# First norm by blocks in the input stage, and five sixths of the modulation weights loaded and multiplied inside the differential heads

## The chip, the cores and the metric

One core of a Trainium2 chip runs the whole program. The metric is the device time of one execution in microseconds (us), lower is better; a comparison is made between runs of two kernels on the same chip.

## The reference, cut to what matters

A two-layer trunk works on 1,024 latent tokens and 128 context tokens of width 1,024, in float32. Layer 0 mixes tokens by differential attention (8 heads), layer 1 by grouped-query attention; each is followed by a gated feed-forward with a short convolution. All norms are modulated:

```python
def adaln_params(cond, mod_w, mod_b):
    m = jax.nn.silu(cond) @ mod_w + mod_b
    return jnp.split(m[:, None, :], N_MOD, axis=-1)
def modulate(x, norm_w, shift, scale):
    return rms_norm(x, norm_w) * (1.0 + scale) + shift
def layer(x, cond, l, rope, ctx_kv):
    sh_a, sc_a, g_a, sh_f, sc_f, g_f = adaln_params(cond, mod_w[l], mod_b[l])
    o, k, v = token_mixer(modulate(x, norm_attn[l], sh_a, sc_a), l, rope, ctx_kv)
    x = x + g_a * o
    f = conv_ffn(modulate(x, norm_ffn[l], sh_f, sc_f), w_up[l], conv_w[l], conv_b[l], w_down[l])
    return x + g_f * f, k, v
```

`mod_w` is 2 x 1,024 x 6,144 floats (48 MB), multiplied with two conditioning vectors. Before the first attention only the shift and scale of the first norm are needed, the first third of layer 0's columns. The first gate is needed after the differential attention, the rest later.

## The kernel before, in words

The program is a row of stages (`build`, L135): `phase_input`, `phase_norm(g, 0)`, `phase_diff_attention`, a trunk stage, the second attention, a second trunk stage. Each stage has one instruction list for each engine: TensorE (PE), VectorE (DVE), ScalarE (ACT), GpSimd (POOL) and SyncE (SP, which issues DMAs). Each list is executed in its order; semaphores tie the engines together, and a stage ends with a barrier.

**Modulation (`phase_input`, L203).** SP loads `mod_w` in 48 slices of 1 MB: six parts ("sixths") `s` of 2,048 columns, each in 8 slices `k` of 128 rows (L244), four buffers in turn. PE multiplies each slice with the conditioning column in four matmuls of 32 x 512 side by side in one PSUM bank (L313). After 8 slices ACT copies the sum, PE transposes it and DVE adds the bias (L345). Between the parts PE transposes the tokens (L299) that POOL loads.

**First norm (`phase_norm`, L371).** Squares on ACT, their sums on DVE, a root on POOL, then `Hh` (ACT, L392) and `Hl` (POOL, L428), the high and low halves of the normed input, for all 1,152 tokens at a time.

**Products.** A float32 product is three matmuls (`product`, L450): high times high, low times high, high times low. Weights arrive in `g.wr`, ACT rounds them to `g.wh` (`w_hi`, L1358), POOL subtracts to get `g.wl` (`w_lo`, L1453). One bank is 24 matmuls of 128 x 384 (`linear_bank`, L457), and a projection (q, k or v of one head) has three banks, ("W", x, n).

**Heads (`phase_diff_attention`, L1195).** `first` computes k, q, v of head 0 and a bank of head 1; then each head is a `body` of ten steps, `s` = 0 to 9. In a step PE does the scores of token tile `s` (`scores_by_rows`, L1560), the transposes of the probabilities of tile `s-1` ("T", L1186), one projection bank of the next head, and in some steps weighted values ("PV"), mean squares ("ST"), broadcasts of roots ("BC"), transposes of cached and new keys. All but the scores use two PSUM banks in turn; `Ring` (L66) numbers the uses, and `wait_free` waits until the use two earlier has been read out. DVE does maxima, rotary steps (`rope`) and `combine` (the difference of the two softmaxes). ACT does exponentials and read-outs. POOL does, in this order within a step:

```python
for s in range(STEPS):
    for p in ST_AT.get(s, []):       # s = 3, 5, 7, 9
        root(ring, p)                # waits for DVE's mean square
    for p in BC_AT.get(s - 1, []):   # s = 5, 7, 9
        store(ring, h, p, not ahead)
    if ahead and s in (1, 4):
        w_lo(after(h, 1), W_HI_AT[s])
    if ahead2 and s == 7:
        w_lo(after(h, 2), "k")
```

ACT does `w_hi` at the end of its steps 1, 4 and 7, behind the read-out of that step's projection bank. The heads 0 to 5 are three rounds of a loop (`Fori`) over two heads, so their waits compare with registers; heads 6 and 7 stand behind it. `g.wr` has two slots, filled in turn. The keys and queries are rotated through two buffers, `rk` and `rq`, that DMAs fill with swapped halves (`rope_swap`, L1131).

Of the kernel before, what the change touches and what calls it, by code (L numbers as in the profile page):

```python
# [134 lines left out]
def build(nc, a):  # L135
# [3 lines left out]
    g.nc, g.a, g.stack, g.norm_sems = nc, a, ctx, {}  # L139
    with ctx:  # L140
# [8 lines left out]
        g.mod = sb("mod", [P, 2 * NMOD, 2])  # L149
        g.coef = sb("coef", [P, 4, KC, 2])  # L150
# [50 lines left out]


def phase_input(g):  # L203


    nc, a, PS = g.nc, g.a, g.PS
    b, stack = scope(g, "in", {
        "rows": ([P, 5, P], F32), "xn": ([P, 3, D], F32), "sc": ([P, KC, 32], F32),
        "mw": ([P, 4, 2048], F32), "mrow": ([P, 2, 512], F32), "lrow": ([P, 4, DH], F32),
        "lprod": ([P, 2, DH], F32), "lsum": ([P, 2], F32), "lexp": ([P, 2], F32)},  # L210
        "zeroed rows_in lam_in x_in0 x_in1 x_in2 mw0 mw1 mw2 mw3 const par_t par_e silu x_t x_e mw_used mod_row mod_t mod_e coef"
        " lam_steps lam_exp", reused=True)
    xin = [b.x_in0, b.x_in1, b.x_in2]
    mw_in = [b.mw0, b.mw1, b.mw2, b.mw3]
    with stack, nc.Block() as block:
        @block.sync
        def _(sp):
            sp.wait_ge(b.zeroed, 1)
            R = b.rows
            loads = [  # L220
                (R[PC_C:PC_C + 8, 0, :], a.c.rearrange("b (k p) -> (b k) p", p=P)),
                (R[PC_CTX:PC_CTX + 8, 0, :], a.c_ctx.rearrange("(k p) -> k p", p=P)),
                (R[PC_NA:PC_NA + 16, 0, :], a.norm_attn.rearrange("l (k p) -> (l k) p", p=P)),
                (R[PC_NF:PC_NF + 16, 0, :], a.norm_ffn.rearrange("l (k p) -> (l k) p", p=P)),
                (R[PC_FIN:PC_FIN + 8, 0, :], a.final_norm.rearrange("(k p) -> k p", p=P)),
                (R[PC_SUB:PC_SUB + 1, 0, :], a.subln_diff),
                (R[PC_QN:PC_QN + 1, 0, 0:DH], a.q_norm_gqa), (R[PC_QN:PC_QN + 1, 0, DH:P], a.q_norm_gqa),
                (R[PC_KN:PC_KN + 1, 0, 0:DH], a.k_norm_gqa), (R[PC_KN:PC_KN + 1, 0, DH:P], a.k_norm_gqa),
                (R[0:96, 1, :], a.mod_b.rearrange("l (k p) -> (l k) p", p=P)),
            ]  # L230
# [16 lines left out]
        @block.scalar  # L247
        def _(act):
            act.wait_ge(b.par_e, 1)
            for cond, col in ((0, PC_C), (1, PC_CTX)):  # L250
                last = act.activation(b.sc[:, :, cond], g.par[:, col:col + KC], ACT.Silu)
            last.then_inc(b.silu, 1)
            for s in range(6):
                act.wait_ge(b.mw_used, KC * (s + 1))
                if s >= 2:
                    act.wait_ge(b.mod_t, s - 1)
                act.activation(b.mrow[:, s % 2, :], PS[:, 2 + s % 2, :], ACT.Copy).then_inc(b.mod_row, 1)
            act.wait_ge(b.lam_steps, 3)
            act.activation(b.lexp[:, :], b.lsum[:, :], ACT.Exp).then_inc(b.lam_exp, 1)

        @block.gpsimd
        def _(pool):
            pool.memset(b.rows[:, :, :], 0.0).then_inc(b.zeroed, 1)
            pool.memset(g.ident[:, :], 0.0).then_inc(b.const, 1)
            pool.memset(b.sc[:, :, :], 0.0).then_inc(b.const, 1)
            pool.memset(g.ones_d[:, :], 1.0 / D).then_inc(b.const, 1)
            pool.memset(g.ones_v[:, :], 1.0 / P).then_inc(b.const, 1)
            pool.memset(g.half[:, :], -0.5).then_inc(b.const, 1)
            pool.memset(g.ones_h[:, :], 0.0).then_inc(b.const, 1)
            pool.memset(g.one[:, :], 1.0).then_inc(b.const, 1)  # L270
            pool.wait_ge(b.const, 7)
            pool.affine_select(out=g.ident[:, :], in_=g.ident[:, :], compare_op=ALU.not_equal, fill=1.0,
                               base=0, pattern=[[-1, P]], channel_multiplier=1).then_inc(b.const, 1)
            pool.wait_ge(b.const, 8)
            pool.memset(g.ones_h[0:DH, 0:1], 1.0 / DH).then_inc(b.const, 1)
            pool.wait_ge(b.const, 9)
            pool.memset(g.ones_h[DH:P, 1:2], 1.0 / DH).then_inc(b.const, 1)

            for t in range(TT):
                if t >= 3:  # L280
                    pool.wait_ge(b.x_t, 2 * (t - 2))
                src = a.x_sample[0, t * P:(t + 1) * P, :] if t < QT else a.x_prompt[0, :, :]
                pool.dma_start(b.xn[:, t % 3, :], src).then_inc(xin[t % 3], 16)

        @block.tensor
        def _(pe):
            pe.wait_ge(b.const, 10)
            pe.wait_ge(b.rows_in, 16 * 15)
            for i in range(5):
                last = pe.transpose(PS[:, i // 4, (i % 4) * P:(i % 4 + 1) * P], b.rows[:, i, :], g.ident[:, :])  # L290
            last.then_inc(b.par_t, 1)

            def x_tile(t):
                pe.wait_ge(xin[t % 3], 16 * (t // 3 + 1))
                for hf in range(2):
                    if t:
                        pe.wait_ge(b.x_e, 2 * (t - 1) + hf + 1)
# [4 lines left out]

            for t in range(3):
                x_tile(t)
            pe.wait_ge(b.silu, 1)
            for s in range(6):
                if s >= 2:
                    pe.wait_ge(b.mod_row, s - 1)
# [2018 lines left out]
```

## Time and profile before

| | before |
|---|---|
| median of 3 runs | 3683.11 us (3680.57 to 3684.28) |
| profiled execution, its own time | 3682.36 us |
| its span, first to last instruction | 3680.7 us |
| TensorE matmuls busy | 3358.0 us (91%) |
| VectorE / ScalarE / GpSimd busy | 1834.0 (50%) / 1181.1 (32%) / 963.7 us (26%) |
| mean granted TensorE clock | 0.949 of full speed |
| read from / written to HBM | 181.79 / 31.98 MB |

The own time holds 1.7 us around the span. In the profile, "idle before" is the time in which an engine waited ahead of an instruction, with the instruction of another engine that released it; the granted clock is 1.00 at 2.4 GHz and 0.50 at 1.2 GHz. Matmul ends are modelled and overlap, so the distance of two starts is the better measure of their pace.

### The profile page before, as it was taken

What the parts mean: (1) busy time and instruction counts of PE and PEld (TensorE: products, weight loads), DVE (VectorE), ACT (ScalarE), POOL (GpSimd) and SP (SyncE); (2) the same over time, 40 slices, a digit from 0 to 9 for tenths busy, and PEclk for the clock granted to TensorE, in tenths of its full rate; (3) what the DMA queues carried; (4) which work ended last, traced back from release to release, by engine and by line L of the source; (5) the groups of instructions that cost most, each with busy time, mean ns of one, the idle gap of its engine ahead of it and who ended that gap; (6) DMA issues with size and microseconds to landing.
All of it is one profiled execution on the core that took longest, in us unless ns stands there. A gap on an engine that the chain in (4) does not pass through costs nothing. (4 is left out here: it accounts for less than half of the span.)

```text
span 3680.7 us, 52758 instructions
## 1 busy us (share of the span) xinstructions
PE 3358.0 (91%) x20815; PEld 3086.4 (84%) x20815; DVE 1834.0 (50%) x2580; ACT 1181.1 (32%) x2085; POOL 963.7 (26%) x732
## 2 busy tenths in 40 slices
PE   5469999998799999999988899999898999999997
PEld 1168888887699999999988777877688999999996
DVE  0345555555335555545545455555516554555554
ACT  0224444444323122221224455555513212122121
POOL 0122222222142233222324122222133322233221
PEclk7689999999899999999999999999899999999998
DMA  9621111111311111111102211111221111111101
GB/s 386 268 61 47 44 45 45 45 45 55 143 36 57 41 40 42 49 36 38 40 29 84 50 30 28 30 26 36 98 92 42 55 42 40 34 40 51 40 29 58
DMA packets 200897, 229.80 MB, mean 62 GB/s; under 512 B 29924, under 2 KB 172893, under 8 KB 194461
## 3 DMA queue, kind: packets, MB, share of 16 engines
q1 hardware_dynamic: 192733, 204.64, 17.3%
q0 software_dynamic: 7856, 22.29, 1.7%
q8 instruction: 122, 2.00, 0.2%
q10 hardware_dynamic: 144, 0.52, 0.0%
q14 instruction: 42, 0.34, 0.0%
HBM read 181.79 MB, written 31.98 MB: 58 GB/s over the span
## 5 line engine op out<-in xcount | busy, mean ns | idle before, releaser
L452 PE MATMUL psum<-Hh,wh 128*128 128x384 f32 x3360 | 1141.3, 340 | 73.8 <-POOL wl L1453 38.2
L454 PE MATMUL psum<-Hl,wh 128*128 128x384 f32 x3360 | 1129.9, 336 | 0.0
L453 PE MATMUL psum<-Hh,wl 128*128 128x384 f32 x3360 | 1129.7, 336 | 0.0
L533 DVE SCALAR_TENSOR_TENSOR x<-psum,mod,x 128x384 f32<-128x384 f32 (+2 forms) x768 | 377.3, 514 | 686.1 <-PE psum L454 642.0
L452 PEld LDWEIGHTS psum<-Hh,wh 128*128 128x128 f32 x3360 | 636.2, 189 | 83.3 <-POOL wl L1453 38.5
L453 PEld LDWEIGHTS psum<-Hh,wl 128*128 128x128 f32 x3360 | 636.1, 189 | 0.0
L454 PEld LDWEIGHTS psum<-Hl,wh 128*128 128x128 f32 x3360 | 635.7, 189 | 0.0
L827 POOL TENSOR_TENSOR wl<-wr,wh 128x1024 fp32r<-128x1024 f32 x88 | 219.7, 2496 | 986.6 <-ACT wh L746 986.6
L777 ACT ACTIVATE ff_u<-psum 128x768 f32<-128x768 f32 x88 | 71.6, 813 | 1109.1 <-PE psum L454 1109.1
L452 PE MATMUL psum<-ff_ah,ff_dh 128*128 128x384 f32 x1056 | 365.2, 346 | 29.4 <-POOL ff_al L849 20.7
L975 DVE SCALAR_TENSOR_TENSOR ff_c<-ff_u,par,ff_c 128x1153 f32<-128x1153 f32 x176 | 377.3, 2144 | 15.7 <-DVE ff_c L972 5.2
L454 PE MATMUL psum<-ff_al,ff_dh 128*128 128x384 f32 x1056 | 357.0, 338 | 0.0
L453 PE MATMUL psum<-ff_ah,ff_dl 128*128 128x384 f32 x1056 | 356.7, 338 | 0.0
L452 PEld LDWEIGHTS psum<-ff_ah,ff_dh 128*128 128x128 f32 x1056 | 199.4, 189 | 47.6 <-POOL ff_al L849 21.3
L2246 DVE TENSOR_REDUCE ga_nm<-psum 128x1 f32<-128x1152 f32 x144 | 177.9, 1235 | 113.3 <-PE psum L2121 113.3
L1604 DVE TENSOR_REDUCE da_nb<-psum 128x1 f32<-128x1152 f32 x144 | 171.6, 1233 | 112.1 <-PE psum L1560 112.1
L972 DVE TENSOR_SCALAR ff_c<-ff_u,par 128x1153 f32<-128x1153 f32 x88 | 81.9, 931 | 286.4 <-ACT ff_u L779 286.4
L2134 PE MATMUL psum<-ident,ga_e 128*128 128x128 f32 x1168 | 182.1, 303 | 39.1 <-ACT ga_e L1957 35.7
L2134 PEld LDWEIGHTS psum<-ident,ga_e 128*128 128x128 f32 x1168 | 142.3, 153 | 78.8 <-ACT ga_e L1957 44.7
L453 PEld LDWEIGHTS psum<-ff_ah,ff_dl 128*128 128x128 f32 x1056 | 200.3, 190 | 0.0
L454 PEld LDWEIGHTS psum<-ff_al,ff_dh 128*128 128x128 f32 x1056 | 199.8, 189 | 0.0
L1957 ACT ACTIVATE ga_e<-psum,ga_nb,ga_r 128x1152 f32<-128x1152 f32 x144 | 174.8, 1216 | 43.4 <-DVE ga_nb L2250 40.3
(208 smaller groups left out, 4216.0 us busy)
## 6 DMA issues: line engine op xcount, KB each, us to landing
in_mw<-mod_w SPq DMA_DIRECT2D x48, 1024.0 KB, 8.8
wr<-w_up SPq DMA_DIRECT2D x88, 512.0 KB, 3.9
ff_dr<-w_down SPq DMA_DIRECT2D x22, 1024.0 KB, 6.0
wr<-w_qkv_diff SPq DMA_DIRECT2D x24, 512.0 KB, 3.9
x<-x_save SPq DMA_DIRECT2D x16, 576.0 KB, 9.1
Hh<-oh_save SPq DMA_DIRECT2D x14, 576.0 KB, 9.6
Hl<-ol_save SPq DMA_DIRECT2D x14, 576.0 KB, 10.5
x_save<-x_a SPq DMA_DIRECT2D x1, 4608.0 KB, 13.6
```

The costliest lines, as they stand in the source:

```text
L452: pe.matmul(out, w_hi, m_hi, start=start, stop=False)
L453: pe.matmul(out, w_lo, m_hi, start=False, stop=False)
L454: return pe.matmul(out, w_hi, m_lo, start=False, stop=stop)
L533: last = dve.scalar_tensor_tensor(g.x[:, m, lo:hi], g.PS[:, bank, lo - n * NB:hi - n * NB], g.mod[:, gate + m, cond:cond + 1], g.x[:, m, l ...
L777: act.activation(u[:, 1:1 + 2 * NB].rearrange("p (n t) -> p n t", n=2), PS[:, s:s + 2, 0:NB], ACT.Copy)
L827: pool.tensor_tensor(g.wl[:, j % 2, :, :], g.wr[:, j % 2, :, :], g.wh[:, j % 2, :, :].bitcast(F32), ALU.subtract).then_inc(b.w_lo, 1)
L972: dve.tensor_scalar(c, u[:, 0:PADT], tap(0), bias, ALU.mult, ALU.add).then_inc(b.conv, 1)
L975: dve.scalar_tensor_tensor(c, u[:, step:step + PADT], tap(step), c, ALU.mult, ALU.add).then_inc(b.conv, 1)
L1604: dve.reduce_max(b.nb[:, m:m + 1], banks(g, m, t), AX.XY if t < QT else AX.X, negate=True).then_inc(b.nmax, 1)
L1957: act.activation(like_banks(b.e[:, m, :], t), banks(g, m, t), ACT.Exp, bias=b.nb[:, m:m + 1], scale=b.r[:, j % 2, t, m:m + 1], accum_out=b ...
L2134: last = pe.transpose(out[:, c, :], b.e[:, m, (c0 + c) * P:(c0 + c + 1) * P], g.ident[:, :])
L2246: dve.reduce_max(b.nm[:, m:m + 1], banks(g, m, t), AX.XY if t < QT else AX.X, negate=True).then_inc(b.mx, 1)
```

## The change

The input stage loads and multiplies only the first sixth (8 slices), and also does the first norm, block by block of 384 tokens (class `Norm`, which the trunk already used: `scale` and `low` on DVE, `high` on ACT). The squares are summed by ACT as the tokens arrive. It also loads the first two weight units and does four of the first six projection banks. `phase_norm` is gone.

The other five sixths (`SLICES`) move into heads 0 to 4. Steps 1 to 8 of such a head begin on PE with a use ("M", s-1): four matmuls with slice `k = s-1`, ahead of the scores. DVE reads it out and adds it up (`accumulate`), ahead of the maxima of that step. Step 9 begins with the transposes ("MT"), and DVE adds the bias. The slice has one buffer: half in `b.mw`, half in slot 1 of `g.wr`. POOL issues the two DMAs of the next slice as the last thing of its step, once PE has used the last one. The weights of the heads therefore have slot 0 of `g.wr` alone. The loop over heads is written out, waits are on constants, the rotary buffers become one (`rot`), and `ck` takes the place of `ko`.

```diff
 def phase_input(g):
-            for s in range(6):
-                for k in range(KC):
-                    i = s * KC + k
-                    if i >= 4:
-                        sp.wait_ge(b.mw_used, i - 3)
-                    sp.dma_start(b.mw[:, i % 4, :], a.mod_w[s // 3, k * P:(k + 1) * P, (s % 3) * 2048:(s % 3 + 1) * 2048])\
-                        .then_inc(mw_in[i % 4], 16)
+            for k in range(KC):
+                if k >= 4:
+                    sp.wait_ge(b.mw_used, k - 3)
+                sp.dma_start(b.mw[:, k % 4, :], a.mod_w[0, k * P:(k + 1) * P, mod_columns(0)]).then_inc(mw_in[k % 4], 16)
+                if k == 3:
+                    for j, col in enumerate(HEAD_UNITS):
+                        sp.dma_start(g.wr[:, j, :, :], wq[:, :, col * P:(col + 1) * P]).then_inc(w_in[j], 16)
...
+            for n in range(2):
+                nf.ready(pe, n)
+                for j in range(2):
+                    if n == 0:
+                        pe.wait_ge(b.w_lo, j + 1)
+                    last = linear_bank(g, pe, AHEAD_BANKS[n][j], g.wh[:, j], g.wl[:, j], n)
...
+            for n in range(NN):
+                for k in range(KC):
+                    nf.scale(dve, n, k)
+                    if k:
+                        nf.low(dve, n, k - 1)
+                nf.low(dve, n, KC - 1)
-def phase_norm(g, which):
...
 def phase_diff_attention(g):
-        "rk": ([P, NS], F32), "rq": ([P, NS], F32),
+        "rot": ([P, NS], F32), "mw": ([P, 2, 512], F32), "acc": ([P, 512], F32),
+    SLICES = 5
+    mw = [b.mw[:, 0, :], b.mw[:, 1, :]] + [g.wr[:, 1, 4 * j:4 * j + 4, :].rearrange("p k n -> p (k n)") for j in range(2)]
...
+            return [("MT",)] * (h < SLICES) + last
+        return [("M", s - 1)] * (h < SLICES) + u
-        with eng.Fori(0, HEADS // 2 - 1) as i:
-            for odd in range(2):
-                body(Head(2 * i + odd, i, odd), Ring(len(FIRST) + odd * len(BODY), 2 * len(BODY), BODY, i), True, True)
+        for h in range(HEADS):
+            body(Head(h, h % 2), Ring(BEFORE[h], 0, USES[h], 0), h + 1 < HEADS, h + 2 < HEADS)
...
             def swap_queries(h, ring):
+                sp.wait_ge(b.rope, 2 * ROPE_STEPS * h.index + 3)
...
+            def load_slice(h, k):
+                s = h + 1
+                rows = a.mod_w[s // 3, k * P:(k + 1) * P, mod_columns(s)]
+                pool.dma_start(b.mw[:, :, :].rearrange("p j n -> p (j n)"), rows[:, 0:1024]).then_inc(b.mw_in, 16)
+                pool.dma_start(g.wr[:, 1, :, :].rearrange("p k n -> p (k n)"), rows[:, 1024:2048]).then_inc(b.mw_in, 16)
...
                     if not ahead and s in (2, 3):
                         first_out_weights_lo(g, pool, b, s - 2)
+                    if ("M", s - 1) in step_uses(h.index, s) and (h.index, s) != (SLICES - 1, STEPS - 2):
+                        pool.wait_ge(b.full, ring.done(("M", s - 1)))
+                        load_slice(h.index + (s == STEPS - 2), s % KC)
...
+                if what == "M":
+                    k = use[1]
+                    ring.wait_free(pe, free, use)
+                    pe.wait_ge(b.mw_in, 32 * (KC * h.index + k + 1))
+                    for j in range(4):
+                        last = pe.matmul(PS[32 * j:32 * j + 32, bank, :], g.sc[:, k, :], mw[j], start=True, stop=True)
+                    last.then_inc(b.full, 1)
+                    return
```

Three places show the order. On POOL, steps 1 to 5 of a head before the change (`da_r` is the root, `wl` is `w_lo`, `da_yh` and `da_yl` are the split of an output that is then stored):

```order
L1453 TENSOR_TENSOR wl<-wr,wh 128x1024
L95 ISA
L1459 TENSOR_TENSOR da_r<-da_ms,half 128x2
L1452 REGISTER_ALU
L1453 TENSOR_TENSOR wl<-wr,wh 128x1024
L95 REGISTER_ALU
L1459 TENSOR_TENSOR da_r<-da_ms,half 128x2
```

POOL now, from the load of step 2 to the start of step 5's store (a load is the pair of DMA rows):

```order
L1451 DMA da_mw<-mod_w 128x1024
L1452 DMA wr<-mod_w 128x1024
L1457 TENSOR_TENSOR da_r<-da_ms,half 128x2
L1451 DMA da_mw<-mod_w 128x1024
L1452 DMA wr<-mod_w 128x1024
L1444 TENSOR_TENSOR wl<-wr,wh 128x1024
L1451 DMA da_mw<-mod_w 128x1024
L1452 DMA wr<-mod_w 128x1024
L1457 TENSOR_TENSOR da_r<-da_ms,half 128x2
L273 TENSOR_TENSOR da_yh<-da_y,one 128x256
```

In step 3 the load stands behind the root, in step 4 behind `w_lo`, in step 5 behind root, split and store.

On PE, the end of step 1 and the start of step 2 before the change (L452 to L454 the projection bank, L1560 the scores):

```order
L452 MATMUL psum<-Hh,wh 128x384
L453 MATMUL psum<-Hh,wl 128x384
L454 MATMUL psum<-Hl,wh 128x384
L1555 ISA
L1560 MATMUL psum<-da_nkh,da_nqh 128x384 [waits in_lam_steps]
L1560 MATMUL psum<-da_nkh,da_nqh 128x384
```

The same place now (the semaphores in brackets have the names of an earlier stage that used them; `in_mw1` is `mw_in`, the landing of the slice, and the other is the ring's):

```order
L205 MATMUL psum<-Hh,wh 128x384
L206 MATMUL psum<-Hh,wl 128x384
L207 MATMUL psum<-Hl,wh 128x384
L1513 MATMUL psum<-da_mw,sc 32x512 [waits in_mw1,in_x_in1]
L1513 MATMUL psum<-da_mw,sc 32x512
L1513 MATMUL psum<-wr,sc 32x512 x2
L1576 MATMUL psum<-da_nkh,da_nqh 128x384 [waits in_const]
```

The four matmuls of the slice stand between the projection bank and the scores, and the first of them waits for the slice's two DMAs.

## Rows read from the trace of the kernel before

**Rows 1.** Busy times by stretch: us, engines, granted clock, DMA share, GB/s.
```profile
147.30:201.90 54.60, 8.21 (x36) 7.83 (x36) 37.01 (x32) 22.09 (x24) 22.79 (x9) 0.53 0.20 87
...
254.60:902.40 647.80, 609.24 (x3915) 544.99 (x3914) 368.84 (x520) 305.18 (x618) 156.81 (x187) 0.99 0.17 42
```
**Rows 2.** PE's waits from 300 to 840 us: total, times, longest.
```profile
PE psum L1512 <- issue: 6.5, 2, 3.4
```
**Rows 3.** Timeline of the input stage: start, duration, instruction, idle before.
```profile
36.69 1.83 PE L313 MATMUL psum<-in_mw,in_sc 128*32 128x512 f32 x8 [0.54 <-DMA in_mw<-mod_w]
...
141.38 1.06 PE L313 MATMUL psum<-in_mw,in_sc 128*32 128x512 f32 x8 [0.54 <-DMA in_mw<-mod_w]
...
142.37 1.09 PE L299 MATMUL psum<-ident,in_xn 128*128 128x128 f32 x8
```
**Rows 4.** Groups by form, the trunk's norm on DVE: busy, mean ns.
```profile
L646 DVE SCALAR_TENSOR_TENSOR Hl<-ff_c,mod,Hh 128x384 fp32r<-128x384 f32 x48 | 40.6, 847 | 3.7 <-ACT Hh L622 3.7
...
L634 DVE SCALAR_TENSOR_TENSOR ff_c<-x,coef,psum 128x384 f32<-128x384 f32 x48 | 29.0, 612 | 1.2
```
**Rows 5.** Timeline from the first projections to the first scores.
```profile
224.18 5.67 SPq L1131 DMA_DIRECT2D da_rk<-da_k  x8
...
231.74 1.22 DVE L1142 TENSOR_TENSOR da_k<-da_k,da_cos 128x1024 f32<-128x1024 f32 x1 [20.58 <-DMA da_rk<-da_k]
...
254.64 0.45 PE L1560 MATMUL psum<-da_nkh,da_nqh 64*128 64x384 f32 x2
```
**Rows 6.** Timeline of head 1, first and last matmul of a projection bank.
```profile
357.60 0.44 PE L452 MATMUL psum<-Hh,wh 128*128 128x384 f32 x1
...
361.69 0.34 PE L454 MATMUL psum<-Hl,wh 128*128 128x384 f32 x1
```
**Rows 7.** Timeline of head 1: starts of PE's steps 2, 4, 5, 6, 8, and POOL.
```profile
361.96 0.44 PE L1560 MATMUL psum<-da_nkh,da_nqh 64*128 64x384 f32 x2
...
363.59 2.36 POOL L1453 TENSOR_TENSOR wl<-wr,wh 128x1024 fp32r<-128x1024 f32 x1 [2.94 <-ACT wh L1358]
...
382.17 0.44 PE L1560 MATMUL psum<-da_nkh,da_nqh 64*128 64x384 f32 x2
...
382.33 0.72 POOL L1459 TENSOR_TENSOR da_r<-da_ms,half 128x2 f32<-128x2 f32 x1 [16.38 <-DVE da_ms L1618]
...
394.10 0.38 ACT L1363 ACTIVATE da_o<-psum 128x256 f32<-128x256 f32 x1
...
394.16 0.44 PE L1560 MATMUL psum<-da_nkh,da_nqh 64*128 64x384 f32 x2
...
395.51 2.37 POOL L1453 TENSOR_TENSOR wl<-wr,wh 128x1024 fp32r<-128x1024 f32 x1 [12.46 <-ACT wh L1358]
...
402.16 0.45 PE L1560 MATMUL psum<-da_nkh,da_nqh 64*128 64x384 f32 x2
...
406.34 0.54 POOL L526 DMA_DIRECT2D ol_save<-da_yl  x1
...
422.20 0.33 PE L1560 MATMUL psum<-da_nkh,da_nqh 64*128 64x128 f32 x2
...
426.31 1.72 POOL L522 TENSOR_TENSOR da_yl<-da_y,da_yh 128x256 fp32r<-128x256 f32 x1
...
429.84 2.36 POOL L1453 TENSOR_TENSOR wl<-wr,wh 128x1024 fp32r<-128x1024 f32 x1
```
**Rows 8.** DMA issues up to 210 us: KB each, median us from issue to landing.
```profile
wr<-w_qkv_diff SPq DMA_DIRECT2D x3, 512.0 KB, 4.0
...
da_sin<-rope_sin POOLq DMA_DIRECT2D x1, 512.0 KB, 5.4
```
**Rows 9.** POOL's issue of a 512 KB load: ns min/median/max.
```profile
L283 POOL DMA_DIRECT2D in_xn<-x_sample x8: 527/531/744, 2.9 to 61.7; - x8
```
**Rows 10.** Busy times behind two waits of PE, as in rows 1.
```profile
261.00:266.00 5.00, 4.99 (x26) 4.23 (x27) 2.39 (x4) 0.87 (x3) 0.00 (x0) 0.50 0.09 26
...
448.00:451.20 3.20, 3.20 (x20) 2.74 (x18) 0.00 (x0) 0.49 (x1) 0.85 (x2) 0.50 0.16 44
```

More of the change, by code:

```diff
@@ L654, in ready, with mod_columns, add_mod_bias @@
         pe.wait_ge(self.b.lo_d, self.k0 + KC * (n + 1))
+HEAD_UNITS = [HEADS, 0]
+AHEAD_BANKS = ((0, 2), (1, 3))
+def mod_columns(s):
+    return slice((s % 3) * 2048, (s % 3 + 1) * 2048)
+def add_mod_bias(g, dve, s, src):
+    for cond in range(2):
+        last = dve.tensor_tensor(
+            g.mod[:, 16 * s:16 * s + 16, cond].rearrange("p (j k) -> p j k", j=4),
+            src.rearrange("p (k j c) -> p c j k", k=4, j=4)[:, cond],
+            g.par[:, PC_MB + 16 * s:PC_MB + 16 * s + 16].rearrange("p (j k) -> p j k", j=4), ALU.add)
+    return last
@@ L1356, in w_hi @@
             def w_hi(h, x):
-                act.wait_ge(w_in[slot(h, x)], loaded(h, x))
-                act.activation(g.wh[:, slot(h, x), :, :], g.wr[:, slot(h, x), :, :], ACT.Copy).then_inc(b.w_hi, 1)
+                act.wait_ge(b.w_in, 16 * (unit(h, x) - 1))
+                act.activation(g.wh[:, slot(h, x), :, :], g.wr[:, 0, :, :], ACT.Copy).then_inc(b.w_hi, 1)
             def copy_out(ring, use, dst, cols, parts=1, scale=1.0):
@@ L1367, in project @@
                 dst, off = {"k": (b.k, PAST), "q": (b.q, 0), "v": (b.vt, 0)}[x]
-                copy_out(ring, use, dst[:, off + n * NB:off + (n + 1) * NB], NB, scale=SCALE if x == "q" else 1.0)
+                dst, scale = dst[:, off + n * NB:off + (n + 1) * NB], SCALE if x == "q" else 1.0
+                if ring is None:
+                    act.activation(dst, PS[:, AHEAD[use], 0:NB], ACT.Copy, scale=scale).then_inc(b.ahead, 1)
+                else:
+                    copy_out(ring, use, dst, NB, scale=scale)
             def softmax(h, t):
@@ L1626, in normalise, with accumulate @@
                                          ALU.mult, ALU.mult).then_inc(free[ring.bank(use)], 1)
+            def accumulate(ring, h, k):
+                use = ("M", k)
+                dve.wait_ge(b.full, ring.done(use))
+                src = PS[:, ring.bank(use), :]
+                if k == 0:
+                    done = dve.tensor_copy(b.acc[:, :], src)
+                else:
+                    ring.wait_read(dve, free, ("M", k - 1))
+                    done = dve.tensor_tensor(b.acc[:, :], b.acc[:, :], src, ALU.add)
+                done.then_inc(free[ring.bank(use)], 1)
             def first(ring):
@@ L1651, in body @@
                         mean_square(ring, p)
+                if h.index < SLICES:
+                    dve.wait_ge(b.full, ring.done(("MT",)))
+                    add_mod_bias(g, dve, h.index + 1, PS[:, ring.bank(("MT",)), :]).then_inc(free[ring.bank(("MT",))], 1)
                 for p in BC_AT[TILES - 1]:
@@ L1661, in _ @@
             heads(dve, first, body)
+            for i in range(1, 4):
+                coefficients(g, dve, i)
 def broadcast_heads(g, pe, out, r):
```

531 lines of the change are left out of this document (251 added, 280 removed).

## The prediction, made before any run of the changed kernel

> **What bounds the kernel now.** I read the busy times by stretch first, then PE's waits, then the timeline of one head. The eight heads but the last run from 254.6 to 902.4 us, and in these 647.8 us PE's matmuls are busy for 609.2 at full clock, DVE for 368.8, POOL for 156.8: PE bounds this part, and whatever PE waits for there is added to the end [rows 1]. Two of its waits, 6.5 us together, have no other engine behind them: they are the turns of the loop over heads [rows 2]. Ahead of the heads PE hardly works: in the 54.6 us of the first norm it is busy for 8.2 [rows 1], and before that it waits for slices of `mod_w` that arrive every 2.5 us [rows 3]. So a slice's product costs nothing in the input stage, where DMA is the bound, and costs its full PE time in a head.
>
> **1. The start, about 140 us gained.** The eighth slice's product began at 36.69 us and ended by 38.5 [rows 3]. The new stage has 2.6 MB more in front of that point (three token tiles, two weight units), less what was then in flight for the second sixth; I add 5 us: 43.5. Read-out, transposes, bias and coefficients take 2.5 more, so the norm starts at 46. Its DVE pair costs 612 + 847 ns per chunk of 128 x 384 in the trunk [rows 4]: eight chunks 11.7 us, two blocks 23.4, the third, cut in two pieces for the two conditions, 13.2 (an estimate). DVE is done at 82.6, and with 1 us for the change of stage the heads' stage starts at 83.6. PE has done four banks by then under DVE's cover, and the first weights' conversion is hidden too. A bank is 4.2 us [rows 6].
>
> Behind it the chain to the first scores is: last k bank 4.2 and 1.3 for a slow clock, read-out 0.5, swap DMA 7.6 (issue 224.18, DVE starts 231.74), three rotary steps 3.7, and only then the q swap, since there is one buffer, 7.7, five steps 6.0: 31.0 us, scores at 114.7. PE's six banks end at 110.9, so the shared buffer shows by 4 us. Before, the first scores were at 254.64 [rows 5]. Gain 140; bounds 128 (the loads 6 us later, DVE slower) and 148 (DVE's second operation at 612 ns).
>
> **2. The loop written out, 10 us gained.** 6.5 us of waits [rows 2], and behind each a stretch of 3.2 us at half clock, which costs 1.6 [rows 10]. Bounds 6 and 12.
>
> **3. The products in the heads, 50 us lost.** At full clock a slice takes 1.0 us (141.38 to the next PE operation at 142.37) [rows 3]; 40 slices are 40 us, five "MT" of 0.6 are 3. "M" stands ahead of the scores and needs the bank of the use two earlier. In steps 3 and 7, and for "MT", that is a "PV" result whose read-out by ACT ends after PE has finished the step: 394.10 + 0.38 against 394.16, so 0.3 to 0.8 us [rows 7]; I take 1.3 per head, 6.5 in all. DVE's 40 additions of 0.7 us lie in the 1.8 us of scores that follow, while DVE waits for them; they are hidden, and would delay the maxima if `combine` ran late. POOL's own time for the DMAs and SP's waits on the single weight slot are hidden: weights are needed steps later.
>
> **4. The single slice buffer behind POOL's other work, 240 us lost.** This decides. Slice `s` can only be loaded when PE has used slice `s-1` at the start of step `s`, and PE needs it at the start of step `s+1`. A step lasts 8 to 12 us, so the load has time, but POOL issues it as the last act of its step. What stands ahead of it ends after PE's step, and `root` and `w_lo` wait for the step's last products. From head 1, where POOL becomes free against PE's start of the next step [rows 7]:
>
> - step 1, `w_lo`: 363.59 + 2.36 = 365.95 against 361.96: 4.0 us late
> - step 3, root: 382.33 + 0.72 against 382.17: 0.9
> - step 4, `w_lo`: 395.51 + 2.37 against 394.16: 3.7
> - step 5, root, split, store: 406.34 + 0.54 against 402.16: 4.7
> - step 7, root, split, store, `w_lo`: 429.84 + 2.36 against 422.20: 10.0, of which I take off 1.3, since the split at 426.31 ran slowly beside a busy DVE, which will be idle: 8.7
>
> Together 22.0 us. Steps 2, 6 and 8 have nothing ahead; those loads are hidden. To each of the five comes the load itself: 0.5 for the first issue [rows 9] and a landing of 512 KB, with half of it still on the way, between 4.0 and 5.4 us [rows 8]. I take 4.7, nearest to the POOL load, which had rivals; 5.2 in all. Bounds 4.5 and 6.0. A head waits 22.0 + 26.0 = 48.0 us, five heads 240; bounds 222 and 260. The scores, and with them DVE and ACT, queue behind PE's wait, so nothing catches up but small waits, 3 us in all.
>
> The Trainium skill ("DMA: Bandwidth & Descriptors", Anatomy of one DMA — SWDGE path) gives 2.0 us plus bytes over 436 GB/s for a load from POOL. By it, as an estimate, the issue of 0.5, one load of 3.2 and 1.2 for the first half's transfer ahead of it, 4.9 us, would stand for my 5.2, and the sum would be 8 us lower. The trace's landings lie above that formula's single load.
>
> **5. The clock, 50 us lost.** After a wait of 3.7 us PE ran 5.0 us at 1.2 GHz, after one of 3.4 us 3.2 [rows 10]. Five waits per head of 6 to 14 us should each do so; the slow time costs half its length, 1.6 to 2.5, and I take 2.0, times 25. Bounds 30 and 75.
>
> **Sum.** 3680.7 - 140 - 10 + 49.5 + 240 - 3 + 50 = 3867.2 for the span, 3869 with the 1.7 us around it. The profiled execution's own time is 0.8 us below the median of the runs, so it serves for both: 186 us, or 5%, slower than before.
>
> **The rivals.**
>
> *The loads are in time (faster).* If POOL issued each slice early enough, by `w_hi` and `w_lo` running in the middle of their steps, terms 4 and 5 vanish: 3680.7 - 140 - 10 + 49.5 = 3580, 3582 with what is around it. For it: the weights are there well before ACT rounds them. Against it: ACT's list has `w_hi` behind the read-out of the step's bank, and POOL waited 2.94 us for it at 363.59 [rows 7]. The point at which the sign turns is 100.5 us for both terms, 20 us a head, against my 57. Chance 0.04.
>
> *PE's clock stays low.* If the slow stretch behind each wait is 10 us, since the waits follow each other every 8 to 22 us, it costs 5 instead of 2: 75 more, 3944. For it: heads at 60% PE share are unlike the ones before. Against it: both stretches in the rows end within 5 us of dense work [rows 10]. Chance 0.10.
>
> *POOL is slowed by DVE.* The split at 426.31 took 1.72 us where its like take 0.7, 2.4 times as long [rows 7]. If that held for both DMA issues, 0.5 us each [rows 9], each late load would be 1.5 us later: 25 x 1.5 = 38, 3907. Against it: at these points DVE has nothing left to do. Chance 0.06. The Trainium skill ("SBUF — State Buffer", the box on DVE blocking a DMA) says that a DMA issued by GpSimd cannot write its descriptors while VectorE holds the shared port. It puts 3.1 us in place of 0.6; by that the price would be 5 us per load, 125 in all. The issues in the trace, 527 to 744 ns, show no such thing.
>
> *Only half of it comes.* Loads land faster (4.0) and the chains ahead of them shrink when the engines around POOL are idle: 35 us a head instead of 48, and 1.5 for the clock: 3867 - 65 - 12 = 3790, 3792. Chance 0.12.
>
> **How the numbers follow.** My forecast has 0.68. The time is its own, 3869. Bounds of its terms one by one: -18 and +20 for the loads, -20 and +25 for the clock, -8 and +12 for the start; they won't all fall on one side, and the range takes in most of the rival at 3792 and the one at 3907: 3800 to 3935. What can be told from no change here is 0.2%, 7 us: faster has the first rival's 0.04 and 0.01 for what I have not seen, same 0.01, slower the rest.
>
> **What would show it.** The first scores near 115 us; no gap at the loop's turns. In the heads 0 to 4 PE waits ahead of the slice's first matmul, with a DMA of `da_mw` or `wr` as releaser, five times a head: some 9, 6, 9, 10 and 14 us, in steps 2, 4, 5, 6 and 8, and none of note in steps 3 and 7. These heads last some 158 us against 92, the heads 5 and 6 stay at 90. The slices' issues stand on POOL right behind `w_lo`, a root or a store. If these waits are under 4 us each, step 4 is wrong and the kernel is faster; if the five heads' waits are right and the clock is low for more than 5 us behind each, the second rival holds; a first score after 130 us would make step 1 wrong.

## The result and the profile after

The changed kernel takes 3917.18 us (median of 4 runs, 3912.03 to 3921.8); the kernel before took 3681.84 us beside it (4 runs, 3678.99 to 3684.28). The ratio is 1.0635, 95% interval 1.0622 to 1.0647: slower by 235 us. The prediction said slower, 3869 us, 3800 to 3935. The profiled execution has a span of 3912.2 us, 231.5 more than before. I read it in the same order as before.

PE's waits from 115 to 960 us, in which heads 0 to 4 run (total, times, longest):

```profile
PE psum L1513 <- DMA wr<-mod_w: 276.5, 25, 15.4
PE psum L1175 <- ACT da_pt L1350: 8.2, 33, 0.3
PE psum L1513 <- ACT da_o L1350: 5.0, 10, 0.6
```

The first row is new, and it is the change: 25 waits for a slice, five in each of five heads, 55.3 us a head. No other wait of PE in this stretch comes near it. The two turns of the loop, 6.5 us [rows 2], are gone.

The timeline of PE in head 2 (counted from 0, as everywhere), steps 2, 3, 4, 5, 6 and 8:

```profile
476.12 1.07 PE L1513 MATMUL psum<-da_mw,sc 128*32 128x512 f32 x2 [10.93 <-DMA wr<-mod_w]
...
492.31 0.62 PE L1513 MATMUL psum<-da_mw,sc 128*32 128x512 f32 x2 [0.64 <-ACT da_o L1350]
...
508.04 1.07 PE L1513 MATMUL psum<-da_mw,sc 128*32 128x512 f32 x2 [6.03 <-DMA wr<-mod_w]
...
534.39 1.07 PE L1513 MATMUL psum<-da_mw,sc 128*32 128x512 f32 x2 [11.01 <-DMA wr<-mod_w]
...
558.34 1.07 PE L1513 MATMUL psum<-da_mw,sc 128*32 128x512 f32 x2 [12.20 <-DMA wr<-mod_w]
...
598.80 1.06 PE L1513 MATMUL psum<-da_mw,sc 128*32 128x512 f32 x2 [15.29 <-DMA wr<-mod_w]
```

A matmul behind such a wait lasts 1.07 us, one behind a short wait 0.62: PE comes out of the long waits at half clock.

The same head on POOL:

```profile
466.75 2.33 POOL L1444 TENSOR_TENSOR wl<-wr,wh 128x1024 fp32r<-128x1024 f32 x1 [3.03 <-ACT wh L1345]
469.03 0.57 POOL L1451 DMA_DIRECT2D da_mw<-mod_w  x1
...
502.62 0.57 POOL L1451 DMA_DIRECT2D da_mw<-mod_w  x1
...
526.94 0.57 POOL L1451 DMA_DIRECT2D da_mw<-mod_w  x1
...
549.75 0.54 POOL L279 DMA_DIRECT2D ol_save<-da_yl  x1
550.28 0.54 POOL L1451 DMA_DIRECT2D da_mw<-mod_w  x1
...
589.45 2.35 POOL L1444 TENSOR_TENSOR wl<-wr,wh 128x1024 fp32r<-128x1024 f32 x1
591.73 0.56 POOL L1451 DMA_DIRECT2D da_mw<-mod_w  x1
```

Each wait falls into two parts at the start of this issue. The first is how late POOL comes: PE was ready at 476.12 - 10.93 = 465.19, POOL issued at 469.03, 3.8 us later. The second is the load: 469.03 to 476.12, 7.1 us. For the five waits:

| wait in step | 2 | 4 | 5 | 6 | 8 | sum |
|---|---|---|---|---|---|---|
| POOL late, us | 3.8 | 0.6 | 3.6 | 4.1 | 8.2 | 20.4 |
| forecast | 4.0 | 0.9 | 3.7 | 4.7 | 8.7 | 22.0 |
| load, us | 7.1 | 5.4 | 7.5 | 8.1 | 7.1 | 35.1 |
| forecast | 5.2 | 5.2 | 5.2 | 5.2 | 5.2 | 26.0 |

Over all 25 waits the same subtraction gives 102.7 us for POOL (forecast 110) and 173.7 us for the load (forecast 130). So POOL's part was right, a little high, and the load's was too low. SP's queue in the same head tells what is beside it:

```profile
469.11 0.38 SPq L1270 DMA_DIRECT2D wr<-w_qkv_diff  x1
...
527.01 0.39 SPq L1270 DMA_DIRECT2D wr<-w_qkv_diff  x1
...
546.41 4.95 SPq L1120 DMA_DIRECT2D da_rot<-da_q  x8
591.83 0.38 SPq L1270 DMA_DIRECT2D wr<-w_qkv_diff  x1
```

At three of the late points SP issues 512 KB of weights within 0.1 us of the slice's load. That is no chance: the weights now have one slot, `w_lo` frees it, and POOL's next act behind the same `w_lo` is the slice. At the fourth (550.28) the swap of the queries and the two stores are under way. Only the load at 502.62 has no such company, and it takes 5.4 us. The other heads repeat this: from issue to PE's start it is 5.4 to 5.5 us for the wait in step 4, 6.8 to 7.5 in steps 2, 5 and 8, and 7.6 to 8.1 in step 6. Busy times by stretch while PE waits in steps 2 and 4 (columns as in rows 1, the last two the share of the DMA engines' time and GB/s):

```profile
470.00:475.00 5.00, 0.00 (x0) 0.00 (x0) 0.00 (x0) 0.00 (x0) 0.14 (x1) 0.50 0.94 307
504.00:508.00 4.00, 0.00 (x0) 0.00 (x0) 0.00 (x0) 0.00 (x0) 0.00 (x0) 0.79 0.77 257
```

With the weights beside it the DMA engines are busy for 94%: the load shares them with bytes that nobody waits for yet, while all compute engines stand still.

The page of the profile, transfers (KB each, median us from issue to landing):

```profile
da_mw<-mod_w POOLq DMA_DIRECT2D x40, 512.0 KB, 4.7
wr<-mod_w POOLq DMA_DIRECT2D x40, 512.0 KB, 6.2
```

Busy times by stretch, columns as in rows 1: the heads up to 1,000 us; then 5 us behind the waits of steps 2 and 8:

```profile
115.00:1000.00 885.00, 575.00 (x3385) 465.20 (x3386) 312.40 (x453) 240.69 (x484) 155.37 (x220) 0.82 0.23 71
```

```profile
477.00:482.00 5.00, 5.00 (x30) 3.57 (x23) 1.42 (x2) 0.00 (x0) 1.05 (x2) 0.50 0.42 123
...
600.00:605.00 5.00, 5.00 (x21) 4.22 (x18) 3.95 (x9) 0.81 (x4) 1.05 (x2) 0.50 0.50 158
```

PE is busy for 65% of the heads' stretch, at 94% before, and the granted clock is 0.82 instead of 0.99 [rows 1]. To size the clock I summed PE's busy time at half clock over windows of 1 us: 129.6 us from 114 to 960, against 12.8 in heads 0 to 4 before. Half of each is the time lost at most: 64.8 against 6.4.

The start, timeline:

```profile
50.74 0.61 DVE L401 SCALAR_TENSOR_TENSOR Hl<-in_full,mod,Hh 128x384 fp32r<-128x384 f32 x1
...
112.25 0.45 PE L1576 MATMUL psum<-da_nkh,da_nqh 64*128 64x384 f32 x2 [1.41 <-DVE da_nql L1139]
```

The first scores are at 112.25, before at 254.64 [rows 5]: 142.4 us earlier. From the first transposes of `vt` of one head to those of the next (L1512 before, L1528 now), heads 0 to 4 take 845.8 us (114.02 to 959.85) against 467.2 (256.43 to 723.60). Heads 5 and 6 take 90.6 and 88.5, as before. So 142.4 us are won at the start, 378.7 lost in five heads, and from head 5 to the end 4.7 less. That part does the same work in all kernels here, and its length in their traces scatters from 2947.5 (ACT-issued loads, below) to 2957.1 us (before), so these 4.7 us are scatter.

### The profile page after: what moved, and what is told of

Its sections match the earlier page's. It is cut to its first block and busy times, and to the rows that moved or that the text cites. A ratio compares the mean times of both kernels' runs of the same rounds, so it can differ in the third digit from the quotient of the medians.

```text
span 3912.2 us, 51583 instructions
## 1 busy us (share of the span) xinstructions
PE 3386.0 (87%) x20797; PEld 3110.2 (80%) x20797; DVE 1853.6 (47%) x2655; ACT 1182.6 (30%) x2106; POOL 979.3 (25%) x806
## 5 line engine op out<-in xcount | busy, mean ns | idle before, releaser
L1513 PE MATMUL psum<-da_mw,sc 128*32 128x512 f32 x160 | 64.7, 896 | 281.5 <-DMA wr<-mod_w 276.5
L1350 ACT ACTIVATE da_pt<-psum 128x384 f32<-128x384 f32 (+1 forms) x200 | 90.2, 481 | 413.3 <-PE psum L1175 412.5
## 6 DMA issues: line engine op xcount, KB each, us to landing
in_mw<-mod_w SPq DMA_DIRECT2D x8, 1024.0 KB, 11.4
```

Of the source, the lines that this page charges most:

```text
L1350: act.activation(dst, src.rearrange("p (n t) -> p n t", n=parts) if parts > 1 else src, ACT.Copy, scale=scale)\
L1513: last = pe.matmul(PS[32 * j:32 * j + 32, bank, :], g.sc[:, k, :], mw[j], start=True, stop=True)
```

## The experiments

Two theories stood against each other. **The issue is late** (mine): POOL's order makes the 25 waits, the load is short enough for a step of 8 to 12 us, and with the issue ahead of POOL's other work the kernel beats the one before. **The load is the matter** (the rival): one buffer and a load of 7 to 8 us bound the heads wherever the issue stands, or PE's added work eats the gain.

**The load as POOL's first act of a step.**

```diff
                 for s in range(STEPS):
+                    if ("M", s - 1) in step_uses(h.index, s) and (h.index, s) != (SLICES - 1, STEPS - 2):
+                        pool.wait_ge(b.full, ring.done(("M", s - 1)))
+                        load_slice(h.index + (s == STEPS - 2), s % KC)
                     for p in ST_AT.get(s, []):
                         root(ring, p)
...
-                    if ("M", s - 1) in step_uses(h.index, s) and (h.index, s) != (SLICES - 1, STEPS - 2):
-                        pool.wait_ge(b.full, ring.done(("M", s - 1)))
-                        load_slice(h.index + (s == STEPS - 2), s % KC)
```

> POOL issues each slice's load as the first act of its step instead of the last; nothing else changes. If the waits come from POOL's order, the 276 us ahead of the slices' products shrink to under 20 us, the 58 us of extra half clock go with them, and the time is 3575 to 3600 us, some 90 us under the kernel before. If the loads themselves are too slow or POOL cannot keep up, waits of several us stay in the short steps (2, 4, 6, 8) and the time stays above 3700 us.

Measured: 3617.9 us (3613.26 to 3622.43), ratio 0.9835 (0.982 to 0.985), 299 us less than with the change as it is (294 by the two ratios). The move of three lines turns 6.4% slower into 1.6% faster, so the place of the load in POOL's order is the cause. The time is 18 us above the upper end of what I expected. PE's waits from 112 to 960 us still have

```profile
PE psum L1513 <- DMA wr<-mod_w: 20.5, 9, 4.2
```

Four of the nine are in step 2, of 2.3 to 4.2 us, and POOL's timeline shows where they come from:

```profile
229.03 0.39 POOL L273 TENSOR_TENSOR da_yh<-da_y,one 128x128 fp32r<-128x128 f32 x1 [3.92 <-DMA ol_save<-da_yl]
...
230.83 0.54 POOL L279 DMA_DIRECT2D ol_save<-da_yl  x1
231.36 0.55 POOL L1451 DMA_DIRECT2D da_mw<-mod_w  x1
```

These are the last two stores of the head before, behind its step 9. The last split waits 3.92 us for an earlier store to leave its buffer, and the load of step 1 stands behind it; PE then waited 4.12 us at 236.75. I had looked at POOL's order within a head, not across its end.

The other five, of 1.3 to 1.6 us, are in step 6 of each head, here of head 2:

```profile
395.76 0.62 PE L1513 MATMUL psum<-da_mw,sc 128*32 128x512 f32 x2 [1.62 <-DMA wr<-mod_w]
```

This load was issued in time, at 388.39, with 512 KB of weights from SP at 388.46 beside it, and took 7.4 us. In this step even an early load meets the weights.

**Those two stores behind the next head's first load.** On top of the last kernel, for heads 0 to 3:

```diff
+                    if s == 1:
+                        for r0, h0, p in later:
+                            store(r0, h0, p, False)
+                        later.clear()
...
                 for p in BC_AT[STEPS - 1]:
-                    store(ring, h, p, not ahead)
+                    if h.index + 1 < SLICES:
+                        later.append((ring, h, p))
+                    else:
+                        store(ring, h, p, not ahead)
```

> load_first, and the last two output stores of heads 0 to 3 moved on POOL behind the load of the next head's step 1. In load_first 9 waits of 20.5 us are left, with 9 us of half clock more than one_slice: POOL comes to step 1's load 6 us late since it waits for the DMA of the store before. If that is all, the waits vanish and the time is 3588 to 3594 us, that of one_slice, 2.5% under the kernel before. If the waits in step 1 come from the load's own length against a step of 7.7 us, 10 us or more of waits stay: 3605 us or more.

Measured: 3593.17 us (3590.28 to 3603.14), ratio 0.9769 (0.975 to 0.9788); the waits for slices are down to

```profile
PE psum L1521 <- DMA wr<-mod_w: 7.4, 5, 1.7
```

The four waits in step 2 are gone. The five in step 6 stay, and they are not of the stores' making.

**The loads issued by ACT.** The same loads, at the same start of a step, stand in ACT's list; POOL issues none.

```diff
         def _(act):
+            def load_slice(h, k):
...
+                act.dma_start(b.mw[:, :, :].rearrange("p j n -> p (j n)"), rows[:, 0:1024]).then_inc(b.mw_in, 16)
+                act.dma_start(g.wr[:, 1, :, :].rearrange("p k n -> p (k n)"), rows[:, 1024:2048]).then_inc(b.mw_in, 16)
...
                 for s in range(STEPS):
+                    if ("M", s - 1) in step_uses(h.index, s) and (h.index, s) != (SLICES - 1, STEPS - 2):
+                        act.wait_ge(b.full, ring.done(("M", s - 1)))
+                        load_slice(h.index + (s == STEPS - 2), s % KC)
```

> The slices' loads issued by ACT at the start of its step, once the product of the last slice is done, and nothing on POOL. ACT is free of the stores. If POOL's order is the cause, the waits ahead of the products vanish: 3590 us. Rival: ACT's two issues, some 0.8 us in each step, and its wait for the product hold up the read-outs that PE waits for; then 40 x 0.4 us or more is lost and it lies above 3605 us.

Measured: 3590.25 us (3583.51 to 3594.6), ratio 0.9759 (0.974 to 0.9777). PE waits for no slice at all. Three of its waits from 114 to 636 us, in heads 0 to 4, that the kernel before doesn't have:

```profile
PE psum L1513 <- ACT da_o L1357: 6.5, 15, 0.6
PE psum L1175 <- DVE da_y L1648: 4.0, 5, 0.8
...
PE psum L205 <- DVE da_ms L1641: 2.6, 5, 0.5
```

The transfers of its page:

```profile
da_mw<-mod_w ACTq DMA_DIRECT2D x40, 512.0 KB, 3.9
wr<-mod_w ACTq DMA_DIRECT2D x40, 512.0 KB, 4.9
```

The loads land sooner than POOL's 4.7 and 6.2. They also start at other moments, so this does not tell the queue from the neighbours. It makes clear that one buffer is enough and that PE's added work doesn't eat the gain: the rival falls.

**Only the first slice loaded.** All 40 products stay and read the first slice that the heads load.

```diff
-                    if ("M", s - 1) in step_uses(h.index, s) and (h.index, s) != (SLICES - 1, STEPS - 2):
-                        pool.wait_ge(b.full, ring.done(("M", s - 1)))
-                        load_slice(h.index + (s == STEPS - 2), s % KC)
...
-                    pe.wait_ge(b.mw_in, 32 * (KC * h.index + k + 1))
+                    pe.wait_ge(b.mw_in, 32)
```

> The changed kernel with only the first slice of the heads loaded; all 40 products read it, so the modulation of the later parts is computed from the wrong data; the other 39 loads are left out. It prices products, additions and bank waits alone. With my terms 1 to 3: 3683 - 142 - 10 + 50 = 3581 us. If the additions on DVE or the bank waits cost more than I took, 3600 us or more. Against load_first it shows what loads in time still cost: 0 to 10 us.

Measured: 3589.61 us, ratio 0.9751 (0.9736 to 0.9766). Without 39 of the 40 loads the time is the same as with all of them issued by ACT, as far as the two intervals tell, some 9 us; heads 0 to 4 take 519.8 us in its trace and 520.1 in that one. So the transfers themselves, 40 MB beside the heads, cost nothing that shows; the products, the start and the loop alone give 3590, not the 3581 I expected.

**The load ahead of `w_lo` only**, still behind roots and stores (a single run):

```diff
+                    if ("M", s - 1) in step_uses(h.index, s) and (h.index, s) != (SLICES - 1, STEPS - 2):
+                        pool.wait_ge(b.full, ring.done(("M", s - 1)))
+                        load_slice(h.index + (s == STEPS - 2), s % KC)
                     if ahead and s in (1, 4):
                         w_lo(after(h, 1), W_HI_AT[s])
```

> The changed kernel with the load moved ahead of w_lo alone; root and store stay ahead of it. If each step's wait is POOL's lateness plus the load, step 2's and step 5's waits fall from 11 us to 4 or less, step 8's from 15.4 to 11 to 13, and those of steps 4 (6.0) and 6 (12.1) stay: 276 us of waits become 150 to 170, and the time falls by 120 to 145 us with the clock, to 3775 to 3800 us. If the waits are not a sum, they don't fall step by step like this.

Measured: 3791.24 us, within what I expected. Waits over the heads, and those of head 2, steps 2, 4, 5, 6 and 8:

```profile
PE psum L1513 <- DMA wr<-mod_w: 161.0, 19, 12.1
```

```profile
416.15 1.07 PE L1513 MATMUL psum<-da_mw,sc 128*32 128x512 f32 x2 [3.63 <-DMA wr<-mod_w]
...
447.93 1.07 PE L1513 MATMUL psum<-da_mw,sc 128*32 128x512 f32 x2 [6.30 <-DMA wr<-mod_w]
...
463.27 0.62 PE L1513 MATMUL psum<-da_mw,sc 128*32 128x512 f32 x2 [0.30 <-ACT da_o L1350]
...
484.42 1.07 PE L1513 MATMUL psum<-da_mw,sc 128*32 128x512 f32 x2 [12.09 <-DMA wr<-mod_w]
...
520.78 1.07 PE L1513 MATMUL psum<-da_mw,sc 128*32 128x512 f32 x2 [11.33 <-DMA wr<-mod_w]
```

The waits behind `w_lo` alone, in steps 2 and 5, shrink to the stores' 3.63 and to none; those behind a root or a store, in steps 4 and 6, stay at 6.3 and 12.1; step 8, where root and stores stay ahead and `w_lo` doesn't, falls from 15.29 to 11.33: POOL is 2.3 us less late, and the load, no longer beside the weights, 1.6 us shorter. Each wait follows what stands ahead of its load on POOL, one by one.

**The weights' load behind the slice's.** SP waits for the slice of that step to land before it issues the next weights; POOL's order is that of the change.

```diff
+                if h.index < SLICES:
+                    sp.wait_ge(b.mw_in, 32 * (KC * h.index + 2))
                 load_w(after(h, 1), "v")
...
+                    if h.index < SLICES:
+                        sp.wait_ge(b.mw_in, 32 * (KC * h.index + 5))
                     load_w(after(h, 2), "k")
...
+                    if h.index < SLICES:
+                        sp.wait_ge(b.mw_in, 32 * (KC * h.index + 8))
                     load_w(after(h, 2), "q")
```

> The changed kernel, but SP loads each unit of the heads' weights only once the slice that POOL issued at the same moment has landed. The load took 5.1 us in step 3, where nothing else is loaded, and about 7 us in steps 1, 4 and 7, where the end of w_lo releases both. If sharing with the weights' load makes that difference, the waits of steps 2, 5 and 8 fall by 1.5 to 2 us each, 25 us in all: 3890 us. Rival: the length is POOL's queue's own; no change, 3917 us.

Measured: 3874.17 us, ratio 1.052 (1.0499 to 1.0541), 43 us less than with the change. The page, the waits over the heads, and those of head 2, steps 2, 4, 5, 6 and 8:

```profile
da_mw<-mod_w POOLq DMA_DIRECT2D x40, 512.0 KB, 4.2
wr<-mod_w POOLq DMA_DIRECT2D x40, 512.0 KB, 4.9
```

```profile
PE psum L1519 <- DMA wr<-mod_w: 251.1, 25, 13.7
```

```profile
461.87 1.07 PE L1519 MATMUL psum<-da_mw,sc 128*32 128x512 f32 x2 [9.05 <-DMA wr<-mod_w]
...
492.56 1.07 PE L1519 MATMUL psum<-da_mw,sc 128*32 128x512 f32 x2 [6.01 <-DMA wr<-mod_w]
...
516.43 1.06 PE L1519 MATMUL psum<-da_mw,sc 128*32 128x512 f32 x2 [9.14 <-DMA wr<-mod_w]
...
539.29 1.07 PE L1519 MATMUL psum<-da_mw,sc 128*32 128x512 f32 x2 [12.12 <-DMA wr<-mod_w]
...
577.73 1.07 PE L1519 MATMUL psum<-da_mw,sc 128*32 128x512 f32 x2 [13.72 <-DMA wr<-mod_w]
```

The waits of steps 2, 5 and 8 fall by 1.9, 1.9 and 1.6 us; those of steps 4 and 6, which had no weights beside them, stay. Both are as expected. In step 8 the weights alone are held back, in steps 2 and 5 also a 64 KB transfer of keys that stands behind them in SP's list (`da_ck`, `new_k_diff`). So two 512 KB transfers from POOL and one from SP that start together do slow each other, by about a quarter of the load's time: 25.4 us of waits in all. The time falls by more, since I had left the clock out: counted as above, half clock costs 52.7 instead of 64.8 us. Heads 0 to 4 of its trace are 35.9 us shorter, near the sum of 37.5; the rest of the 43 lies within the intervals of the two times, some 9 us. Why 2 us less of a wait should shorten the slow stretch behind it stays open.

**The waits filled.** Ahead of the five late products PE multiplies something of no use into the bank, 56, 28, 56, 62 and 80 matmuls, so that it is busy while the slice is on its way.

```diff
                     ring.wait_free(pe, free, use)
+                    for _ in range({1: 56, 3: 28, 4: 56, 5: 62, 7: 80}.get(k, 0)):
+                        pe.matmul(PS[:, bank, 0:NB], g.Hh[:, 0, 0:P], g.Hh[:, 0, 0:NB], start=True, stop=True)
                     pe.wait_ge(b.mw_in, 32 * (KC * h.index + k + 1))
```

> The changed kernel with 56, 28, 56, 62 and 80 extra matmuls on PE (128 x 384, results overwritten) ahead of the five late products of each head, so that PE is busy during nearly all of the wait. The five loads still end when they did. If the clock costs what the trace shows, 58 us, the time falls by 45 to 60 us to about 3865 us, with the granted clock of the heads near 1. Rival: the slow matmuls are hidden in other waits, then nothing is gained and the time is 3917 us or more.

Measured: 3863.73 us, ratio 1.0504 (1.0488 to 1.0521), 53.4 us less. Waits, and busy times of the heads' stretch:

```profile
PE psum L1515 <- DMA wr<-mod_w: 27.4, 25, 2.3
```

```profile
115.00:1000.00 885.00, 816.94 (x5113) 718.52 (x5111) 342.05 (x498) 263.30 (x532) 175.03 (x239) 1.00 0.25 74
```

The granted clock is 1.00 where it was 0.82, and a kernel with some 1,400 useless matmuls more is faster: by 53 us in the medians, by 48 in the ratios (40 to 56 by their intervals), and by 51.5 in heads 0 to 4 of the traces. That prices the clock: some 50 us for 61.8 counted (64.8 less the 3.0 left), so the count is an upper bound, as said.

**The kernel before, loop written out.**

```diff
-        with eng.Fori(0, HEADS // 2 - 1) as i:
+        for i in range(HEADS // 2 - 1):
```

> The kernel before with the loop over heads written out, nothing else. My term 2: the two PE gaps of 3.1 to 3.4 us go, with the half clock behind them: 8 to 12 us faster, about 3672 us. Rival: the gaps are instruction fetch, which the longer program has too: no change (within 3 us).

Measured: 3676.03 us (11 runs), ratio 0.998 (0.9969 to 0.9991): 7.4 us gained, 3.3 to 11.4 by the interval. In its trace the two waits at the turns are gone, and heads 0 to 4 take 457.8 us instead of 467.2, 9.4 less. So both agree with the 10 I took.

**Two sixths at the start.** While DVE does the norm, PE has room. On top of the ACT-issued loads, the second sixth is loaded and multiplied there too, four slices ahead of block 0's projection banks and four ahead of block 1's, and one head fewer holds products.

```diff
-            for k in range(KC):
+            for k in range(2 * KC):
...
+                for k in (range(KC, KC + 4), range(KC + 4, 2 * KC))[n]:
+                    pe.wait_ge(mw_in[k % 4], 16 * (k // 4 + 1))
+                    for j in range(4):
+                        last = pe.matmul(PS[32 * j:32 * j + 32, 4, :], g.sc[:, k - KC, :],
+                                         b.mw[:, k % 4, j * 512:(j + 1) * 512], start=k == KC, stop=k == 2 * KC - 1)
+                    last.then_inc(b.mw_used, 1)
...
-    SLICES = 5
+    SLICES = 4
```

> On top of scalar_issues (3590.25 us): the second sixth's slices, 8 to 15, are loaded and multiplied in the input stage, while PE idles under the norm, so one head fewer holds products (SLICES = 4). Theory (the start is bound by the norm on DVE, and PE and the DMA have room beside it): a head loses 8 products at 1.0 us and its bank waits, 9 to 11 us, and the start comes 0 to 6 us later, since 8.4 MB more pass beside x_save: 3580 to 3590 us, no DMA wait at the products. Rival (the start is bound by the transfers): the first scores come more than 10 us later than 115, and the time is 3590 to 3605 us.

Measured: 3579.08 us (3575.16 to 3583.2), ratio 0.9731 (0.9717 to 0.9744). The norm starts at 48.21 us as with the change (48.19):

```profile
48.21 1.14 DVE L389 SCALAR_TENSOR_TENSOR in_full<-x_a,coef,psum 128x384 f32<-128x384 f32 x2 [0.25 <-PE psum L368]
```

That is 11 us less than with one sixth, at a start no later. The two intervals just overlap, but the traces agree: heads 0 to 4 take 507.9 us instead of 520.1. This is the fastest version: 338 us less than the change as it stands, 100 less than before. How much of `mod_w` more would fit under the norm wasn't tried.

## Why the prediction was right, and where its sizes were off

The direction, the mechanism and its places were right, and the time lies 48 us above the forecast, in the range. No two large errors cancelled: the two terms that were off, steps 3 and 4, were both too low, by 47 us together. By its steps, against the forecast sum of 3867.2 and the measured span of 3912.2:

| step | forecast | measured | from |
|---|---|---|---|
| 1. start | -140 | -142.4 | first scores, 254.64 to 112.25 |
| 2. loop | -10 | -7.4 | kernel before, written out |
| 3. products | +49.5 | +60.3 | ACT-issued loads |
| 4. late slices | +240 | +276.5 | the 25 waits |
| 5. clock, less small catches | +47 | +49.3 | what is left of the heads' 378.7 |
| from head 5 on | 0 | -4.7 | trace, scatter |

**Step 1 held.** The norm started at 48.2, not 46, but its second DVE operation took 0.61 us, not the 847 ns of the trunk [rows 4]; that was the bound I had named. The same line of the kernel before, with its spread (duration min/median/max over all 96, three widths), shows that the mean was a poor price:

```profile
L646 DVE SCALAR_TENSOR_TENSOR Hl<-ff_c,mod,Hh x96: 344/545/2809, 1086.5 to 2821.1; 128x384 fp32r<-128x384 f32 x48, 128x256 fp32r<-128x256 f32 x24, 128x128 fp32r<-128x128 f32 x24
```

Eight of the 96 operations took 1.2 to 2.8 us and pull it up; the start has none such.

**Step 2** held: 7.4 us by the runs, 9.4 by the trace, and 10 are not told apart.

**Step 3 was 11 us too low.** With no wait for slices, heads 0 to 4 take 520.1 us (vt at 114.16 and 634.22 in the kernel with ACT's loads) against 467.2: 52.9 more with the loop's gain in it, 60.3 without. A slice does take 1.0 us, as I had it: 8.0 a head. What I had too low are the waits for banks. Without the loop's turns, PE waits 22.3 us in heads 0 to 4 of the kernel before and 38.4 here: 16.1 us more, where I took 6.5. To the `da_o` read-outs in steps 3 and 7 and at "MT" come those of step 5, waits for DVE at the transposes (`da_y`, 4.0) and ahead of a projection bank (`da_ms`, 2.6), and short ones for `da_vt` and `da_q`. That leaves 1 to 3 us, as one takes 7.4 or 9.4 for the loop.

**Step 4 named the wrong length for the load; the lateness held.** "5.2 in all" came from a POOL load of the start [rows 8]. A load with no other does take 5.4 (502.62 to 508.04), but four of five share the DMA with the weights that the same `w_lo` releases, or with a swap and stores, and take 6.8 to 8.1. That was to be seen in the diff: the weights had lost their second slot. I had put SP's wait on it down as hidden, since weights are needed steps later. That is true of the weights. It isn't true of the slice whose load they meet. Over the 25 waits the loads took 43.7 us more than forecast and POOL's lateness 7.3 less; that is the 36.5 us between 240 and 276.5. Putting the weights behind the slice took 25.4 back. Another 12.9 belong to the loads ahead of step 6, which it left as they were; that the swap and the stores make those slow is read from the timeline and was not tested. The last 5 us are a load without company at 5.4 to 5.5 instead of 5.2. The formula of the Trainium skill ("DMA: Bandwidth & Descriptors", Anatomy of one DMA — SWDGE (gpsimd) path) gave 4.9 us by estimate, further from what was measured than 5.2.

**Step 5** held in its size: 49 is what the other rows leave of the heads' 378.7, against 47, and the filled waits gave some 50 back. The slow stretch behind a wait is on average as long as the longer of the two, 3.2 and 5.0 us, that I had read [rows 10]: the count gives 129.6 / 25 = 5.2 us of busy time, 2.6 lost each at most, against my 2.0.

**The rivals.** *Loads in time* is what the kernels with an early issue are, 3590 against the 3582 worked out for it; most of the gap is step 3. It took a change to the code: ACT's `w_hi` ran as late as I had read it (POOL waited 3.03 us for it at 466.75, 2.94 before). *Clock low* for 10 us: no, though the sign that I had set for it came true in part. I had written that the rival holds if the clock is low for more than 5 us behind each wait. In the trace it was low for 5.0 to 6.5 us behind the waits of steps 5, 6 and 8, and mostly for 3.0 to 3.5 behind those of steps 2 and 4. The mark stood too near my own 3.2 to 5.0 to tell the two apart; the size does, about 50 us and not 125. *POOL slowed by DVE*: the loads' issues on POOL took 0.53 to 0.57 us in head 2, so my 1.5 us more per load doesn't show. There DVE mostly stood still; but with the load first in its step DVE works during 48 of the 80 issues, and none took over 0.58 us either. Nor does the 3.1 us show that the Trainium skill ("SBUF — State Buffer", A bandwidth-pool intuition that's wrong) reports for a DMA issued by GpSimd beside a DVE copy, and that I had put in for an issue. *Half of it comes*: no, the waits were 55 us a head, not 35; POOL's lateness was 7% under the forecast only, and the loads were longer.

## What to carry to other kernels

With one buffer, the load of the next piece is on the path as soon as its issue comes late. Write down, for the queue that issues it, what stands ahead of the issue and what those things wait for, across the end of the loop body too; a load put first in its step instead of last was worth some 300 us here. Then ask what else the same event releases, since it will share the DMA with the load. And a wait is worth more than its length: 25 waits of 11 us cost 276 us and some 50 more in clock, so that even useless matmuls in them paid.

## What the runs showed of the hardware that was not expected

- 1 MB in two loads from POOL reached PE in 5.4 us with nothing beside it, in 7.1 to 7.5 us with 512 KB of weights issued by SP within 0.1 us (head 2). With the weights held back, the second load's median landing went from 6.2 to 4.9 us. The DMA engines were 77% busy at 257 GB/s in the one case, 94% at 307 GB/s in the other, though the mean over the heads is 71 GB/s: a low mean says nothing of the few microseconds in which a load is waited for.
- Forty loads of 1 MB beside PE-bound heads cost nothing measurable when issued in time: 3590.25 us with them, 3589.61 with one, told apart to some 9 us.
- Some 50 us came back when PE's idle time was filled: granted clock 1.00 for 0.82. Behind the wait of 10.93 us that ended at 476.12 the granted clock was 0.50, 1.2 GHz, until 482, 0.93 from 482 to 485, and 1.00, 2.4 GHz, from 485 to 488.
- One DVE operation (`low`) has a median of 0.545 us over its three widths and single cases of 2.8 us in the trunk. What slows those wasn't tried.
